# Expert rows of a two-block network: two gathers of 4 KB per row become one gather of 8 KB

## The chip, the core and the metric

The kernel runs on one core of a Trainium2 chip. The metric is the time of one execution on the device in microseconds; lower is better. Five engines run their own instruction streams and wait for each other by semaphores: TensorE (PE, matmuls), VectorE (DVE), ScalarE (ACT, activation functions), GpSimd (POOL, here only the issuer of gathers) and SyncE (SP, here only the issuer of plain transfers). Sixteen DMA engines move data between HBM and the on-chip buffers: `arena` (SBUF, 128 partitions) and `ps` (PSUM, the matmuls' accumulators).

## The reference

Two network blocks follow one another on 256 tokens of width 1024. The first has two layers; each mixes tokens (attention, a Fourier and a pooling branch, weighed by sigmoid gates) and then runs a layer of experts, in the first layer for 256 context tokens too. The second block has an attention and a recurrent mixer and one expert layer. Eight tiles of 128 tokens pass through an expert layer. For each token 128 of 16384 experts are chosen; an expert is a row of `peer_down` and a row of `peer_up`, 1024 numbers each:

```python
top_s, pos = lax.top_k(cand, PEER_TOPK)                   # 8 heads x 16 experts a token
eidx = jnp.take_along_axis(cidx, pos, axis=-1)
gate = jax.nn.softmax(top_s, axis=-1)
def one(args):
    hh, ee, gg = args
    a = jnp.einsum("tkd,td->tk", peer_down[ee], hh, preferred_element_type=jnp.float32)
    act = (gg * jax.nn.gelu(a)).astype(hh.dtype)
    return jnp.einsum("tk,tkd->td", act, peer_up[ee])
```

The gates of the mixer that the change also touches:

```python
g = jax.nn.sigmoid((zg + lp["b_gate"]).astype(jnp.float32)).astype(h.dtype)
g_a, g_b, g_c = jnp.split(g, N_BRANCH, axis=-1)
return (g_a * y_a + g_b * y_b + g_c * y_c) @ lp["w_out"], (k, v)
```

## The kernel before

The order of the work is written out by hand. The class `Walk` goes through the whole program; one subclass for each engine (`Vector`, `Tensor`, `Scalar`, `Pool`, `Sync`) goes the same way and issues its own instructions. `weave` lays two sequences into each other: the steps of a gather, and the units of other work (query projections, choice of experts for a later tile, the mixer of the next stage), about one unit (`RATE0` = 1.15) after each step. Since all engines walk the same interleaving, an instruction stands behind everything that its engine issues for earlier steps and units, and waits there for its own semaphores.

An expert layer is a **gather**. There are three: one of four tiles (two of the tokens, two of the context), and two of two tiles, 1024 rows in all. A **row** is one expert for each of the 128 tokens of a tile. Its down rows (128 x 4 KB) are fetched by one indirect DMA and its up rows by another. At step s:

- GpSimd (`Pool.gather`, DMAs recorded at L3075) fetches down row s into one of five buffers (`ND`), once VectorE is through with row s-5, then up row s-18 into one of five others (`NU`), once TensorE, and in odd tiles VectorE, are through with up row s-23 (`freed`).
- VectorE (`Vector.gather`, L906) waits for down row s and multiplies it by the tile's tokens, which lie in PSUM (`HP`), summing along the row: the **dot**, 128x1024 with an accumulator. After each 16 rows (`GK`) it multiplies 16 activated sums by the expert gates `GT`. In odd tiles it also does the **add** of row s-18 (`LAG`): the up row's second half times its weight, onto the sum `av` in PSUM, 128x512.
- ScalarE (`Scalar.gather`, L2462) takes gelu of 16 sums at a time, and for each row scales the identity by the row's weights into one of four 128x128 diagonals (`dg`).
- TensorE (`Tensor.gather`, L1701) multiplies the diagonal with the up row and accumulates into `ap` (first half), in even tiles into `av` too. Each such matmul leaves two records in the trace.
- At the end of a tile VectorE folds both sums, times a row of the modulation, into the tile (`fold`). In the last 18 steps of a gather no down rows are left, and up rows use all ten buffers.

The waits that tie these together, at L3052 and L3069:

```python
if s >= ND:
    self.wait_ge(S.down, c - ND + 1)
...
if i < 0:
    self.freed(max(0, u - NU + 1), total)
```

The gates of the mixer are ScalarE's sigmoids of matmul results, which VectorE multiplies with the branches.

## Time and profile before

| | |
|---|---|
| median of three runs | 4182.21 us (4175.77 to 4186.01) |
| span of the profiled execution | 4362.9 us |
| TensorE, VectorE, ScalarE, GpSimd busy in it | 77%, 59%, 19%, 47% |
| gathers: first indirect DMA of the first one | 446.77 us |
| queue q0 (GpSimd's transfers) | 1141.10 MB in 313344 packets |

The profiled execution is longer than the timed ones; its rows are read against its own span. The page gives each engine's busy time over the whole; the windows give the same for any stretch, with the granted clock of TensorE (1 is full speed) and what the DMA engines moved. The timeline shows single instructions with the idle time of their engine ahead of them and who ended it.

### The profile page before, as it was taken

How to read it: one execution, taken by the hardware profiler on the slowest of the kernel's cores; microseconds unless marked ns; L12 is line 12 of the kernel's file. 1: busy time of each engine (PE TensorE's matmuls, PEld its weight loads, DVE VectorE, ACT ScalarE, POOL GpSimd, SP SyncE). 2: the span in 40 equal slices, each digit the busy share in tenths (PEclk: the TensorE clock that was granted, in tenths of full speed). 3: DMA queues.
4: the chain of work that ended last, by engine and by line, in shares of the span. 5: the costliest groups of instructions: out<-in, count | busy, mean ns of one | idle time of the engine just before them, and what ended most of it. 6: DMA issues, size and time to landing. Idle time of an engine off the chain costs nothing.

```text
span 4362.9 us, 35889 instructions
## 1 busy us (share of the span) xinstructions
PE 3358.4 (77%) x11238; PEld 1715.0 (39%) x11238; DVE 2577.2 (59%) x5454; ACT 816.5 (19%) x1926; POOL 2040.9 (47%) x2148
## 2 busy tenths in 40 slices
PE   6889686888767787887687766766878887866766
PEld 2357442356434243551354422221366654422111
DVE  1412768566686846676357674666563347684776
ACT  1311111321211122121211111111231211111111
POOL 0210566655555666666116665566000005676665
PEclk9999899999979899996899988866988998999556
DMA  6663998999999999999849999999400039999999
GB/s 228 227 237 130 338 363 320 375 356 409 401 362 355 343 378 352 392 410 375 298 159 369 333 365 392 372 405 374 157 1 1 1 113 338 352 350 372 379 369 346
DMA packets 380787, 1330.31 MB, mean 305 GB/s; under 512 B 39500, under 2 KB 44876, under 8 KB 377016
## 3 DMA queue, kind: packets, MB, share of 16 engines
q0 software_dynamic: 313344, 1141.10, 69.3%
q1 hardware_dynamic: 61104, 164.18, 10.1%
q10 hardware_dynamic: 6152, 22.74, 1.4%
q8 instruction: 93, 1.52, 0.1%
q14 instruction: 94, 0.77, 0.1%
HBM read 1326.69 MB, written 1.17 MB: 304 GB/s over the span
## 4 chain that ended last, share of the span: by engine, by line
PE 15%; DVE 10%; DMA 9%; issue 7%; POOL 5%; another core or an unknown queue 3%; ACT 2%; ACTq 0%; DVEq 0%; POOLq 0%
PE ps L1701 15%; POOL arena L3075 5%; DMA arena<-in_peer_up,arena 5%; DVE arena L893 3%; DVE arena L906 3%; DMA arena<-in_peer_v,arena 2%; ACT arena L2462 1%; DMA arena<-in_ada_w 1%; DMA arena<-in_peer_u,arena 1%; DMA arena<-in_peer_down,arena 1%; PE ps L1707 1%; DVE arena L914 1%; DVE arena L1287 1%; DVE arena L1282 0%
## 5 line engine op out<-in xcount | busy, mean ns | idle before, releaser
L1701 PE MATMUL ps<-arena 128*128 128x512 f32 (+9 forms) x10500 | 3254.6, 490 | 873.9 <-ACT arena L2462 231.9
L1701 PEld LDWEIGHTS ps<-arena 128*128 128x128 f32 (+4 forms) x10500 | 1621.6, 196 | 2435.2 <-issue 1844.2
L906 DVE SCALAR_TENSOR_TENSOR arena<-arena,ps 128x1024 f32<-128x1024 f32 x1024 | 1240.6, 1217 | 542.1 <-DMA arena<-in_peer_down,arena 289.1
L3075 POOL DMA_INDIRECT arena<-in_peer_down,arena x768 | 747.1, 973 | 654.8 <-DVE arena L910 269.5
L3075 POOL DMA_INDIRECT arena<-in_peer_up,arena x768 | 736.5, 959 | 541.2 <-PE ps L1701 294.3
L2462 ACT ACTIVATE arena<-arena 128x128 f32<-128x128 f32 (+5 forms) x1242 | 444.4, 387 | 1890.8 <-PE ps L1701 636.3
L3075 POOL DMA_INDIRECT arena<-in_peer_u,arena x256 | 248.4, 970 | 647.9 <-DVE arena L910 543.6
L906 DVE SCALAR_TENSOR_TENSOR ps<-arena,ps 128x512 f32<-128x512 f32 x508 | 383.4, 755 | 143.0 <-DMA arena<-in_peer_up,arena 88.8
L2462 ACT ACTIVATE arena<-ps 128x512 f32<-128x512 f32 (+4 forms) x349 | 191.5, 549 | 1165.6 <-PE ps L1701 547.9
L3075 POOL DMA_INDIRECT arena<-in_peer_v,arena x256 | 242.4, 947 | 149.2 <-issue 59.9
L893 DVE TENSOR_TENSOR arena<-arena 128x512 f32<-128x512 f32 (+8 forms) x398 | 246.9, 620 | 72.1 <-ACT arena L2462 42.1
L893 DVE TENSOR_TENSOR arena<-ps,arena 128x512 f32<-128x512 f32 (+3 forms) x192 | 131.3, 684 | 254.8 <-PE ps L1701 220.8
L1707 PE MATMUL ps<-arena 128*128 128x128 f32 (+2 forms) x738 | 129.6, 314 | 124.5 <-DVE arena L893 68.5
L893 DVE TENSOR_TENSOR arena<-arena,ps 128x256 f32<-128x256 f32 (+1 forms) x134 | 73.0, 545 | 222.7 <-PE ps L1701 171.2
L1707 PEld LDWEIGHTS ps<-arena 128*128 128x128 f32 (+2 forms) x738 | 97.8, 157 | 205.8 <-issue 108.6
L2462 ACT ACTIVATE arena<-ps,arena 128x256 f32<-128x256 f32 (+2 forms) x140 | 71.2, 508 | 423.1 <-PE ps L1701 260.4
L910 DVE COPY arena<-ps 128x512 f32<-128x512 f32 (+5 forms) x69 | 39.6, 574 | 172.2 <-PE ps L1701 124.0
L2462 ACT ACT_TABLE_LOAD x81 | 103.9, 1283 | 56.1 <-DVE arena L893 29.8
L1277 DVE MAX8 arena<-ps 128x8 f32<-128x128 f32 x128 | 28.6, 288 | 137.9 <-PE ps L1701 98.7
L3021 POOL DMA_DIRECT2D arena<-in_w_mod x40 | 30.6, 765 | 132.0 <-PE ps L1701 69.6
L906 DVE DVE_READ_ACCUMULATOR arena<-arena,ps 128x1 f32 x1024 | 86.3, 84 | 0.0
L914 DVE TENSOR_REDUCE arena<-ps 128x1 f32<-128x512 f32 (+2 forms) x50 | 30.3, 607 | 81.9 <-PE ps L1701 69.4
(34 smaller groups left out, 565.1 us busy)
## 6 DMA issues: line engine op xcount, KB each, us to landing
arena<-in_w_mod POOLq DMA_DIRECT2D x40, 1024.0 KB, 6.6
arena<-in_gate_blocks SPq DMA_DIRECT2D x16, 2048.0 KB, 7.8
arena<-in_w_in SPq DMA_DIRECT2D x14, 2048.0 KB, 7.9
arena<-in_w_pq SPq DMA_DIRECT2D x13, 2048.0 KB, 16.0
arena<-in_ada_w POOLq DMA_DIRECT2D x24, 1024.0 KB, 8.3
arena<-in_w_out SPq DMA_DIRECT2D x8, 2048.0 KB, 8.0
arena<-in_gate_blocks SPq DMA_DIRECT2D x8, 1792.0 KB
arena<-mod_scratch ACTq DMA_DIRECT2D x26, 512.0 KB
```

The lines of the kernel that those rows point to most:

```text
L893: self.e.tensor_tensor(o, a, b, op).then_inc(*(inc or self.inc(self.S.vec)))
L906: self.e.scalar_tensor_tensor(o, a, s, b, op0, op1, accum_out=accum).then_inc(*(inc or self.inc(self.S.vec)))
L910: self.e.tensor_copy(o, a).then_inc(*(inc or self.inc(self.S.vec)))
L914: self.e.tensor_reduce(o, a, AX, op).then_inc(*(inc or self.inc(self.S.vec)))
L1277: e.max(v[j][:, 0:8], src[j]).then_inc(*self.inc(S.vec))
L1287: e.match_replace(tmp[j], v[j][:, 0:8], src[j], NEG).then_inc(*self.inc(S.vec))
L1701: return self.e.matmul(o, l, r, start=start, stop=stop)
L1707: ins = self.e.transpose(o, x, self.K.ident)
L2462: self.e.activation(o, i, f, bias=bias, scale=scale, accum_out=accum).then_inc(*(inc or self.inc(self.S.act)))
L3021: self.e.dma_start(K.sums[place].rearrange("p (k n) -> p k n", n=512), rows[:, 4 * half:4 * half + 4, :]).then_inc(S.sums_in[place], 16)
L3075: self.e.indirect_dma_start(out=o, out_offset=None, in_=table, in_offset=bass.IndirectOffsetOnAxis(ap=idx.bitcast(U32), axis=0)).then_inc( ...
```

## The change

The two tables are laid side by side, so that a row of the new table `peer_pairs` holds an expert's down row and up row, 8 KB; for the second block `peer_pairs_2`. One indirect DMA of 128 x 8 KB fetches both into one of six pair buffers (`NP`; 48 KB of a partition, where ten buffers of 4 KB were). A pair is free again when TensorE, and in odd tiles VectorE, are through with its up half. `LAG` falls from 18 to 1: matmul and add of row s-1 stand at step s. ScalarE therefore works row by row: gelu of 128x1, a copy scaled by the expert gate (VectorE's multiplication of 16 columns is gone; a new semaphore `gated` tells ScalarE that the gates are there), the diagonal. `LEAD` = 16 keeps the place where modulation rows are asked for. The fold writes into the row buffer and needs three instructions for four. The mixer's gates become 0.5 (1 + tanh(z/2)): ScalarE takes tanh with scale 0.5 and a halved bias, VectorE (1 + tanh) times the branch in one instruction of the same size, and the 0.5 goes into a later product. The arena is laid out anew and is 6 KB of a partition longer; GpSimd's descriptor scratch gives those up (2048 for 8192). Rates and units of the interleaving stay, apart from marks ("after") that follow the new lag. GpSimd has one gather DMA per row, 512, 256 and 256 in the three gathers, where it had twice as many; ScalarE has 99 table loads where it had 81.

```diff
-ND = NU = 5
-GK = 16
-LAG = GK + 2
+NP = 6
+LAG = 1
+LEAD = 16
...
-    def down_place(self, s):
-
-        x = self.base + LAG // 2 * self.gathers + s
-        return self.K.ds[x % ND], (self.S.down_in[x % ND], 16 * (x // ND + 1))
-
-    def up_place(self, u, total):
-
-        i = u - (total - LAG)
-        if i < 0 or i % 2 == 0:
-            x = self.base - LAG // 2 * self.gathers + (u if i < 0 else total - LAG + i // 2)
-            return self.K.us[x % NU], (self.S.up_in[x % NU], 16 * (x // NU + 1))
-        return self.down_place(total + i // 2)
+    def pair_place(self, s):
+
+        x = self.base + s
+        return self.K.pairs[x % NP], (self.S.pair_in[x % NP], 16 * (x // NP + 1))
...
-            yield ("after", 2 * NEXT + 6)
+            yield ("after", 2 * NEXT + LAG - 12)
...
+        self.ts(K.cols2[:, :, 0:24], K.cols2[:, :, 0:24], 0.5, None, M, None)
...
-                    self.tt(MX[:, j, :], gs[i], b.ap[:, 0:256], M, inc=self.drain(b))
+                    self.stt(MX[:, j, :], gs[i], 1.0, b.ap[:, 0:256], AD, M, inc=self.drain(b))
...
-                self.tt(ty, b.ap, g[:, 512 * c:512 * c + 512], M, inc=self.drain(b))
+                self.stt(ty, b.ap, 0.5, g[:, 512 * c:512 * c + 512], M, M, inc=self.drain(b))
...
-        self.tt(gt, gt, m["s8b"][:, hs].unsqueeze(2).to_broadcast([128, n, 16]), M)
+        self.tt(gt, gt, m["s8b"][:, hs].unsqueeze(2).to_broadcast([128, n, 16]), M, inc=self.inc(S.gated))
...
-                c = base + s
                 if k == 0:
                     self.wait_ge(*self.next(S.row_in_psum))
-                d, there = self.down_place(s)
+                pair, there = self.pair_place(s)
                 self.wait_ge(*there)
+                d = pair[:, 0:D]
                 self.stt(d, d, 1.0, K.HP, M, M, inc=self.inc(S.down), free=True, accum=K.AA[n % 2][:, k:k + 1])
-            if s >= GK + 1 and (s - 1) % GK == 0 and s - 1 <= total:
-                n_, g = divmod((s - 1) // GK - 1, NEXT // GK)
-                ks = slice(GK * g, GK * g + GK)
-                self.wait_ge(*self.next(S.activated))
-                w = K.AW[n_ % 2]
-                self.tt(w[:, ks], w[:, ks], K.GT[:, tiles[n_], ks], M, inc=self.inc(S.weighted), free=True)
-                self.weighted = self.own()
             u = s - LAG
             if u >= 0:
                 n, k = divmod(u, NEXT)
                 c = base + u
-                w = K.AW[n % 2][:, k:k + 1]
-                buf, there = self.up_place(u, total)
                 if n % 2:
-                    self.wait_ge(*there)
-                    if k % GK == 0:
-                        self.wait_ge(*self.weighted)
-                src = buf[:, 512:1024]
-                if n % 2 and self.halves(u):
-                    self.wait_ge(S.up_vector, self.halves(u))
-                if n % 2 == 0:
-                    pass
-                elif k == 0:
-                    self.wait_ge(S.tile_done, c // NEXT)
-                    self.ts(K.av, src, w, None, M, None, inc=self.inc(S.up_vector), free=True)
-                else:
-                    self.stt(K.av, src, w, K.av, M, AD, inc=self.inc(S.up_vector), free=True)
-                if k == NEXT - GK:
+                    src, w = self.pair_place(u)[0][:, D + 512:2 * D], K.AW[n % 2][:, k:k + 1]
+                    self.wait_ge(S.weighted, c + 1)
+                    if self.halves(u):
+                        self.wait_ge(S.up_vector, self.halves(u))
+                    if k == 0:
+                        self.wait_ge(S.tile_done, c // NEXT)
+                        self.ts(K.av, src, w, None, M, None, inc=self.inc(S.up_vector), free=True)
+                    else:
+                        self.stt(K.av, src, w, K.av, M, AD, inc=self.inc(S.up_vector), free=True)
+                if k == NEXT - LEAD:
                     gate = self.row()
                 if k == NEXT - 1:
                     self.fold(tiles[n], c, *gate)
         self.base += total
         self.shared += total // 2
-        self.gathers += 1
 
     def fold(self, t, c, n0, gr, g_in):
 
         K, S = self.K, self.S
         self.wait_ge(*g_in)
         self.wait_ge(S.up_tensor, c + 1)
-        self.tt(K.tpb, K.ap, gr[:, 0:512], M)
-        self.tt(self.X(t)[:, 0:512], self.X(t)[:, 0:512], K.tpb, AD)
-        self.tt(K.tpb, K.av, gr[:, 512:1024], M, inc=self.inc(S.sum_read))
-        self.tt(self.X(t)[:, 512:1024], self.X(t)[:, 512:1024], K.tpb, AD, inc=self.inc(S.tile_done))
+        self.tt(gr[:, 0:512], K.ap, gr[:, 0:512], M)
+        self.tt(gr[:, 512:1024], K.av, gr[:, 512:1024], M, inc=self.inc(S.sum_read))
+        self.tt(self.X(t), self.X(t), gr, AD, inc=self.inc(S.tile_done))
...
-                buf, there = self.up_place(u, total)
-                self.wait_ge(*there)
+                up = self.pair_place(u)[0][:, D:2 * D]
                 if k == 0 and c:
                     self.wait_ge(S.sum_read, c // NEXT)
-                ins = self.mm(K.ap, K.dg[c % 4], buf[:, 0:512], k == 0, k == NEXT - 1)
+                ins = self.mm(K.ap, K.dg[c % 4], up[:, 0:512], k == 0, k == NEXT - 1)
                 if n % 2 == 0:
-                    ins = self.mm(K.av, K.dg[c % 4], buf[:, 512:1024], k == 0, k == NEXT - 1)
+                    ins = self.mm(K.av, K.dg[c % 4], up[:, 512:1024], k == 0, k == NEXT - 1)
                 ins.then_inc(*self.inc(S.up_tensor))
...
-                self.act(g_, b.ap[:, 0:256], ACT.Sigmoid, bias=K.cols2[:, l, 8 * i + j:8 * i + j + 1], inc=self.drain(b))
+                self.act(g_, b.ap[:, 0:256], ACT.Tanh, scale=0.5, bias=K.cols2[:, l, 8 * i + j:8 * i + j + 1], inc=self.drain(b))
...
-            if s >= GK and s % GK == 0 and s <= total:
-                n_, g = divmod(s // GK - 1, NEXT // GK)
-                ks = slice(GK * g, GK * g + GK)
-                self.wait_ge(S.down, base + s)
-                self.act(K.AW[n_ % 2][:, ks], K.AA[n_ % 2][:, ks], gelu, inc=self.inc(S.activated))
-            if s < total and k == 0:
-                if base + s:
-                    self.wait_ge(S.down, base + s)
-                self.act(K.HP[:, 0:512], K.H2[:, tiles[n], 0:512], ACT.Copy)
-                self.act(K.HP[:, 512:1024], K.H2[:, tiles[n], 512:1024], ACT.Copy, inc=self.inc(S.row_in_psum))
-            u = s - LAG + 1
-            if 0 <= u < total:
-                n, k = divmod(u, NEXT)
-                c = base + u
-                if k % GK == 0:
-                    self.wait_ge(*self.next(S.weighted))
+            if s < total:
+                c = base + s
+                if k == 0:
+                    if c:
+                        self.wait_ge(S.down, c)
+                    self.act(K.HP[:, 0:512], K.H2[:, tiles[n], 0:512], ACT.Copy)
+                    self.act(K.HP[:, 512:1024], K.H2[:, tiles[n], 512:1024], ACT.Copy, inc=self.inc(S.row_in_psum))
+                if k in K.routed_at[tiles[n]]:
+                    self.wait_ge(*self.next(S.gated))
+                a, w = K.AA[n % 2][:, k:k + 1], K.AW[n % 2][:, k:k + 1]
+                self.wait_ge(S.down, c + 1)
+                self.act(a, a, gelu, inc=self.inc(S.activated), free=True)
+                self.act(w, a, ACT.Copy, scale=K.GT[:, tiles[n], k:k + 1], inc=self.inc(S.weighted))
                 if c >= 4:
                     self.wait_ge(S.up_tensor, c - 3)
-                self.act(K.dg[c % 4], K.ident, ACT.Copy, scale=K.AW[n % 2][:, k:k + 1], inc=self.inc(S.diagonal), free=True)
+                self.act(K.dg[c % 4], K.ident, ACT.Copy, scale=w, inc=self.inc(S.diagonal))
             u = s - LAG
-            if u >= 0 and u % NEXT == NEXT - GK:
+            if u >= 0 and u % NEXT == NEXT - LEAD:
...
-                c = base + s
-                if k in self.K.routed_at[tiles[n]]:
+                if k in K.routed_at[tiles[n]]:
                     self.wait_ge(*self.next(S.routed))
-                if s >= ND:
-                    self.wait_ge(S.down, c - ND + 1)
-                elif base:
-                    self.freed(0, total)
-                o, there = self.down_place(s)
-                self.fetch(o, down, K.EI[:, tiles[n], k:k + 1], there[0])
-            u = s - LAG
-            if u >= 0:
-                n, k = divmod(u, NEXT)
-                c = base + u
-                i = u - (total - LAG)
-                if i < 0:
-                    self.freed(max(0, u - NU + 1), total)
-                elif i >= ND + NU:
-                    self.freed(u - ND - NU + 1, total)
-                elif i % 2 == 0:
-                    self.freed(total - LAG + i // 2 - NU + 1, total)
-                else:
-                    self.wait_ge(S.down, base + total + i // 2 - ND + 1)
-                o, there = self.up_place(u, total)
-                self.fetch(o, up, K.EI[:, tiles[n], k:k + 1], there[0])
+                self.freed(max(0, s - NP + 1))
+                pair, there = self.pair_place(s)
+                self.fetch(pair, table, K.EI[:, tiles[n], k:k + 1], there[0])
         self.base += total
         self.shared += total // 2
-        self.gathers += 1
-
-    def freed(self, n, total):
+
+    def freed(self, n):
...
-    K.NB = NB = 53200
-    K.arena = arena = ctx.enter_context(nc.sbuf_tensor("arena", [128, NB + 2 * D], F32))
+    K.NB = NB = 52688
+    K.END = END = NB + 4 * D
+    K.arena = arena = ctx.enter_context(nc.sbuf_tensor("arena", [128, END], F32))
...
-    more = Mem(arena, (NB, NB + 2 * D))
-    K.ds, K.us = [gm(D) for _ in range(ND - 1)] + [more(D)], [gm(D) for _ in range(NU - 1)] + [more(D)]
+    tail = Mem(arena, (NB, END))
+    K.pairs = [gm(2 * D) for _ in range(4)] + [tail(2 * D) for _ in range(2)]
...
+    pair = lambda a, b: np.concatenate([np.asarray(inputs[k]).reshape(-1, D) for k in (a, b)], 1)
+    f["peer_pairs"], f["peer_pairs_2"] = pair("peer_down", "peer_up"), pair("peer_u_2", "peer_v_2")
...
-    nc = bacc.Bacc("TRN2", target_bir_lowering=False, num_devices=1, dynamic_dma_scratch_size=8192)
+    nc = bacc.Bacc("TRN2", target_bir_lowering=False, num_devices=1, dynamic_dma_scratch_size=2048)
...
```

What moved on ScalarE in the first gather, where the context attention is laid between the rows. The exps are `128x256`, `128x2x128` is a copy out of PSUM that belongs to them, a diagonal is `128x128`, the batch of 16 gelus `128x16`. Before:

```order
L2462 ACTIVATE arena<-ps 128x2x128
L2462 ACTIVATE arena<-ps,arena 128x256
L2462 ACTIVATE arena<-arena 128x128
L2462 ACTIVATE arena<-ps,arena 128x256
L2462 ACT_TABLE_LOAD
L2462 ACTIVATE arena<-arena 128x16
L2462 ACTIVATE arena<-arena 128x128 x2
```

After, where `128x1 x2` is the gelu and the weight of one row:

```order
L2438 ACTIVATE arena<-arena 128x128
L2438 ACT_TABLE_LOAD
L2438 ACTIVATE arena<-ps,arena 128x256
L2438 ACT_TABLE_LOAD
L2438 ACTIVATE arena<-arena 128x1 x2
```

The gelu stands between every two exps now, and each change of function has its table load.

What moved on VectorE at the end of the first gather. A dot is `arena<-arena,ps 128x1024`, an add `ps<-arena,ps 128x512`, the `TENSOR_TENSOR` rows behind them are the fold (the one of `128x16` is a batch's weights). Before:

```order
L906 SCALAR_TENSOR_TENSOR arena<-arena,ps 128x1024
L906 SCALAR_TENSOR_TENSOR ps<-arena,ps 128x512 x2
L893 TENSOR_TENSOR arena<-arena 128x16
L906 SCALAR_TENSOR_TENSOR ps<-arena,ps 128x512 x17
L893 TENSOR_TENSOR arena<-ps,arena 128x512
L893 TENSOR_TENSOR arena<-arena 128x512
```

After:

```order
L898 SCALAR_TENSOR_TENSOR ps<-arena,ps 128x512
L898 SCALAR_TENSOR_TENSOR arena<-arena,ps 128x1024
L898 SCALAR_TENSOR_TENSOR ps<-arena,ps 128x512 x2
L885 TENSOR_TENSOR arena<-ps,arena 128x512 x2
L885 TENSOR_TENSOR arena<-arena 128x1024
```

The adds that stood behind the last dot are two, where they were nineteen, and the fold follows at once.

## Rows read from the trace of the kernel before

**Rows 1.** Page, part 1: busy us (share of the span) x instructions.

```profile
PE 3358.4 (77%) x11238; PEld 1715.0 (39%) x11238; DVE 2577.2 (59%) x5454; ACT 816.5 (19%) x1926; POOL 2040.9 (47%) x2148
```

**Rows 2.** Windows, gather stages: us, busy us (x count) by engine, PEclk, DMA share, GB/s.

```profile
446.00:2070.00 1624.00, 1277.96 (x3730) 665.33 (x3730) 1094.45 (x2390) 321.77 (x809) 988.85 (x1024) 0.89 0.97 370
2268.00:3070.00 802.00, 573.49 (x1332) 234.30 (x1333) 517.97 (x1075) 124.04 (x314) 494.68 (x512) 0.81 0.97 370
3605.00:4363.00 758.00, 542.43 (x1216) 210.23 (x1216) 511.91 (x1058) 117.09 (x296) 490.77 (x512) 0.78 0.96 360
```

**Rows 3.** Windows, short stretches inside the gathers, same columns.

```profile
1000.00:1100.00 100.00, 87.41 (x320) 60.10 (x319) 67.95 (x115) 20.58 (x51) 60.03 (x64) 0.98 1.02 410
1400.00:1500.00 100.00, 73.05 (x164) 29.45 (x164) 86.78 (x284) 13.74 (x37) 65.73 (x67) 0.90 0.95 348
2915.00:2956.00 41.00, 30.01 (x33) 7.12 (x32) 31.80 (x50) 6.33 (x17) 27.83 (x31) 0.61 1.03 409
4100.00:4200.00 100.00, 70.84 (x72) 17.62 (x72) 70.72 (x110) 13.99 (x37) 66.23 (x71) 0.53 0.98 375
```

**Rows 4.** DMA queues at 1000:1100 us: packets, MB, share of 16 engines.

```profile
q0 software_dynamic: 8923, 32.50, 81.6%
q1 hardware_dynamic: 1472, 8.39, 20.5%
```

**Rows 5.** DMA queues at 1800:1900 us.

```profile
q1 hardware_dynamic: 609, 7.58, 18.2%
```

**Rows 6.** Timeline 4203 to 4206 us: start, us, instruction, [idle before <-releaser].

```profile
4203.23 1.22 DVE L906 SCALAR_TENSOR_TENSOR arena<-arena,ps 128x1024 f32<-128x1024 f32 x1 [1.45 <-issue]
4203.73 0.40 ACT L2462 ACTIVATE arena<-arena 128x128 f32<-128x128 f32 x1 [3.09 <-PE ps L1701]
4203.96 0.94 POOL L3075 DMA_INDIRECT arena<-in_peer_v,arena  x1 [0.98 <-PE ps L1701]
4204.37 0.08 DVE L906 DVE_READ_ACCUMULATOR arena<-arena,ps 128x1 f32 x1
4204.51 0.76 DVE L906 SCALAR_TENSOR_TENSOR ps<-arena,ps 128x512 f32<-128x512 f32 x1
...
4204.62 2.05 PE L1701 MATMUL ps<-arena 128*128 128x512 f32 x2 [1.44 <-ACT arena L2462]
...
4205.21 0.94 POOL L3075 DMA_INDIRECT arena<-in_peer_u,arena  x1 [0.30 <-issue]
```

**Rows 7.** Waits, GpSimd: us in total, times, longest us.

```profile
POOL arena L3075 <- PE ps L1701: 349.7, 230, 10.5
POOL arena L3075 <- DVE arena L906: 193.0, 178, 8.1
```

**Rows 8.** Timeline 446 to 452 us, start of the first gather.

```profile
446.77 1.03 POOL L3075 DMA_INDIRECT arena<-in_peer_down,arena  x1 [194.69 <-DVE arena L910]
...
451.30 1.22 DVE L906 SCALAR_TENSOR_TENSOR arena<-arena,ps 128x1024 f32<-128x1024 f32 x1 [1.22 <-DMA arena<-in_peer_down,arena]
```

**Rows 9.** Groups of ScalarE, shapes apart: busy us, mean ns, idle before.

```profile
L2462 ACT ACT_TABLE_LOAD x81 | 103.9, 1283 | 56.1 <-DVE arena L893 29.8 <-PE ps L1701 14.8 <-issue 3.6
L2462 ACT ACTIVATE arena<-ps,arena 128x256 f32<-128x256 f32 x88 | 41.8, 475 | 386.7 <-PE ps L1701 260.4 <-issue 65.0 <-remote 59.3
...
L2462 ACT ACTIVATE arena<-arena 128x1 f32<-128x1 f32 x68 | 13.8, 203 | 72.9 <-DVE arena L901 43.7 <-DVE arena L893 26.6 <-DMA arena<-in_cvec 0.8
...
L2462 ACT ACTIVATE ps<-arena 128x512 f32<-128x512 f32 x16 | 9.6, 602 | 0.5
...
L2462 ACT ACTIVATION_READ_ACCUMULATOR arena<-ps,arena 128x1 f32 x48 | 9.3, 193 | 0.0
```

**Rows 10.** Waits, VectorE, 446 to 2070 us.

```profile
DVE arena L906 <- DMA arena<-in_peer_down,arena: 147.1, 130, 6.5
...
DVE arena L1277 <- PE ps L1701: 38.2, 6, 9.5
```

**Rows 11.** Timeline 1030 to 1036 us, the gates' stretch.

```profile
1035.86 0.42 DVE L893 TENSOR_TENSOR arena<-arena,ps 128x256 f32<-128x256 f32 x1
```

59 lines of the change are left out of this document (26 added, 33 removed).

## The prediction

> **What bounds the kernel now.** I began with the busy line of the page: no engine is full over the span, TensorE with 77% leads [rows 1]. So the bound changes by stage. The windows by stage come next: three stages hold the 1024 gather rows (446 to 2070, 2268 to 3070, 3605 to 4363 us), 3184 us together, and in each the DMA engines are 96 to 97% busy while TensorE and VectorE are not [rows 2]. A busy share is not yet a rate, so short windows follow [rows 3]: the same full share carries 410 GB/s at 1000:1100 and 409 at 2915:2956, but 375 at 4100:4200 and 348 at 1400:1500, where VectorE is 87% busy with the expert choice. The reader is to see two kinds of rows: some at the DMA's best rate, and some where the buffers do not come back soon enough to hold it.
>
> One row is 1.0486 MB (128 x 8 KB), so at 409 GB/s it lasts 2.56 us. The bytes of the three stages are 1624 x 370 + 802 x 370 + 758 x 360 = 1170 MB; at 409 GB/s they would take 2860 us, so some 324 us of the 3184 lie above that floor.
>
> Everything is summed against the profiled execution of 4363 us. The median of the runs is 4182, 0.9586 of it; no row says where the 181 us lie, so I scale a change by 0.9586.
>
> **Part 1: 8 KB instead of twice 4 KB.** The bytes stay, so only what a packet costs beside its bytes can go. At 1000:1100 queue q0 (gather rows) took 81.6 us x 16 / 8923 = 146.3 ns per packet of 3642 B [rows 4]; at 1800:1900 queue q1 (weights, larger packets) took 18.2 x 16 / 609 = 478 ns per packet of 12,447 B [rows 5]. The line through both is 9.1 ns + 37.7 ns per 1000 B; q1 at 1000:1100 lies on it (223 ns for 5700 B; the line says 224). Two packets of 4096 B then take 327 ns and one of 8192 B takes 318: 2.8% less, 0.071 us per row, **-73 us** over 1024 rows. Bounds: 0, if the row still goes in two packets, and -73, since no row shows more.
>
> The Trainium skill (DMA: Bandwidth & Descriptors, section "Where 436 GB/s comes from") speaks against any gain: it gives about 358 GB/s as the core's share of HBM, and a limit on bytes does not move with packets. The trace disagrees: 409 to 410 GB/s from HBM [rows 3]. By that rule this term would be 0.
>
> **Part 2: one issue per row.** Before, each row costs GpSimd two indirect DMAs of 0.94 us, each followed by 0.30 us [rows 6]: 2.48 us, almost the 2.56 us of the transfer. After a stall it cannot catch up, and it stalls: 349.7 us in 230 waits for TensorE and 193.0 in 178 for VectorE [rows 7], always with the other stream queued behind the one that is stuck. After, an issue of the same kind takes 1.24 us per row. Twice the bytes per descriptor might make it longer; up to 2.5 us it would be hidden. What this returns is the part of the 324 us in which nothing else is late: the gather rows without other work, about 560 us (2900 to 3070, 3923 to 4013, 4050 to 4350), where 375 instead of 409 GB/s [rows 3] costs 8%: **-45 us**. The rows beside the expert choice are bounded by VectorE's own work and I give them nothing. Bounds: 0, and half of the 324, -162.
>
> **Part 3: six pairs, one row of lag.** A pair is held until the matmul of its row is done. First fetch at 446.77, first dot at 451.30: 4.5 us [rows 8]; the second half MB adds 1.28 us at 409 GB/s, so about 5.8 (an estimate). Then dot and its accumulator 1.31, gelu and weight 0.20 each [rows 9], diagonal 0.40, matmuls 2.05 at the low clock [rows 6], and 0.5 for hops: 10.5 us. Six buffers give 1.74 us per row, under 2.5, with 6 x 2.49 - 10.5 = 4.4 us to spare. Before, five down buffers had 5 x 2.56 - 5.8 = 7 us. So a pure row keeps the DMA's pace, and any hiccup beyond 4 us now idles the DMA where 6 to 7 were allowed. Price for pure rows: 0.
>
> **Part 4: the chain closes.** Before, gelu came once per 16 rows and ScalarE, TensorE and the addition worked 18 rows behind; VectorE could dot far ahead of the matmul. In the first gather it waits 147.1 us for the down rows and for TensorE only 6 times worth naming [rows 10]. After, the matmul of row s-1 needs dot s-1 through ScalarE, the other work's matmuls stand behind it in TensorE's order, their readers stand behind on ScalarE and VectorE, and the next dots behind those. As I read the order, this ring spans two rows. In the gates' stretch, 1000:1100, 32 rows in 100 us are 3.1 us per row; of 320 matmul records 64 belong to rows, so the others hold 87.4 x 256/320 = 70 us, 2.2 per row [rows 3]. The ring is dot 1.31 + ScalarE 0.80 + row's matmuls 1.05 + other matmuls 2.2 + VectorE's reader 0.42 [rows 11] + hops 0.5 = 6.3 us per two rows, 3.1 per row: exactly today's pace. In even tiles the row has four records, 0.9 us more, and 0.2 to 0.5 us per row are lost. I take **+20 us**; bounds 0 and +100.
>
> ScalarE itself gets three small instructions per row instead of one: 0.8 us of 2.5, hidden beside its 19% [rows 1]. Not hidden is the context attention: the order puts 16 exps between the rows' gelus, each now with a table load on either side. ScalarE's row there is 2 x 1.283 + 0.475 + 0.19 + 0.80 = 4.0 us against some 2.8: 16 x 1.2 = 19 us [rows 9]; with the ring through the scores' matmuls somewhat more. I take **+25 us**, bounds 0 and +50. In sum the program has 18 loads more (99 for 81), 23 us of ScalarE's time.
>
> First what the row shows: a load is 1283 ns [rows 9]. The Trainium skill (ScalarE: Activation LUTs, section "Table sets: the hidden batching unit") says to batch activations by table set, and names about 2.7 us for a switch; the trace has 1.28 for the load alone. The batches of 16 that are given up kept that rule. By 2.7 us the 32 loads of the attention would add some 45 us to my 25; the tanh gates keep it elsewhere.
>
> **Part 5: small things.** At a tile's end the two copies into PSUM (0.602 each [rows 9]) and the fold now follow the last dot at once instead of 18 rows apart: about 1 us on each of 8 tiles beyond the 4.4 us to spare. The three lead-outs lose their 17 rows of up fetches alone, but the bytes are the same. **+10 us**; bounds 0 and +25. Removed and on no path: 64 weight multiplications of 16 columns, four adds per fold to three. Gates by tanh: one VectorE form for another of the same size, 0.
>
> **Sum:** -73 - 45 + 20 + 25 + 10 = -63 us; 4363 - 63 = 4300; x 0.9586 = **4122 us**, 1.4% less.
>
> **Rivals.** (a) The rows go out no faster: an 8 KB row is moved as two 4 KB packets. For it: no packet of 8 KB on q0 is in the trace, only on q1. Then Part 1 is 0, and the sum +10 us, 4192: no change that can be told. The Trainium skill (DMA: Bandwidth & Descriptors, section "SWDGE vs HWDGE vs iDMA") states packets of at most 4096 B "preferably" on GpSimd's path; no row of before can show it.
>
> (b) **Slower**: the ring closes within one row. If the reader of TensorE's other work stands ahead of the next dot in the same step, the 6.3 us are paid per row, 3.2 more, in the gates' stretches (900 to 1150 and 1750 to 1990: 490 us, 158 rows). All of them would be +500; a quarter, as far as other units lie between and the 4.4 us of slack bridge it, is +125. Then -73 + 0 + 25 + 125 + 10 = +87, 4450 x 0.9586 = 4266. It decides from a fifth of those rows on (-73 - 45 + 35 + 100 is above zero). Against it: DMA share there is already full, and 3.1 us per row leave VectorE a third idle.
>
> (c) More is won: with GpSimd half idle and one stream, half of the 324 us comes back: -73 - 162 + 30 = -205, 4158 x 0.9586 = 3986. For it: VectorE waited for rows 130 times in the first gather alone [rows 10].
>
> **How the numbers follow.** Forecast 0.42 (own range 4080 to 4165), (a) 0.15, (b) 0.28, (c) 0.15. A measurement of this kernel can tell about 0.3%, 12.5 us. Faster: (c) and nearly all of the forecast, 0.55; same: most of (a), 0.15; slower: (b) and a rest of (a), 0.30. The range must reach both (b) and (c), 3985 to 4280.
>
> **What will show it.** q0's packets per MB halve if Part 1 holds, and the full windows read about 420 GB/s; GpSimd's busy time falls by a half, from 2041 to about 1080 us; windows of the last 300 us of gathers 2 and 3 go from 375 towards 410. ScalarE's loads read 99, and the stretch of the context attention is longer by some 25 us. Wrong would be: q0 still with packets of 4 KB; GpSimd's issue at 1.9 us; VectorE's dots waiting for TensorE in the gates' stretch, with the DMA share there under 0.9.

## The result, and the profile after

The changed kernel takes 4213.76 us (median of 4 runs) where the kernel before takes 4178.99: a ratio of 1.0082, 95% interval 1.0067 to 1.0098. It is **slower by 0.8%**, 35 us, and the interval excludes a ratio of 1, where 1.4% faster was forecast. The time lies inside the range of 3985 to 4280, but on the other side of no change.

The first part of the page of the changed kernel, and its largest DMA queue, beside [rows 1]:

```profile
PE 3334.9 (79%) x11238; PEld 1687.5 (40%) x11238; DVE 2541.6 (60%) x5383; ACT 1365.7 (32%) x3928; POOL 1050.5 (25%) x1124
...
q0 software_dynamic: 165888, 1141.03, 68.1%
```

GpSimd's busy time is halved and the packets of q0 fall from 313344 to 165888 with the same bytes, both as foretold. Yet the span of this execution, 4213.8 us, is *shorter* than the 4362.9 us of the trace that the prediction was read from. That alone says that the two traces can't be compared as they stand, so the kernel before was traced once more (first experiment below). That second trace has a span of 4177.6 us, what the timed runs take. From here on "before" is this second trace.

Windows, same columns as [rows 2]. The kernel before, second trace: rows 96 to 127 of the first gather (beside the context attention), the gates' stretch, and gather rows without other work:

```profile
714.00:812.00 98.00, 82.02 (x227) 38.89 (x227) 55.51 (x120) 34.43 (x91) 60.63 (x65) 0.87 0.92 346
965.00:1065.00 100.00, 87.30 (x326) 61.53 (x325) 68.21 (x116) 20.32 (x49) 60.60 (x65) 0.98 1.02 409
...
3985.00:4085.00 100.00, 72.21 (x78) 18.32 (x78) 76.66 (x121) 16.02 (x43) 72.50 (x78) 0.60 1.03 409
```

The changed kernel, the same three places:

```profile
738.00:864.00 126.00, 93.16 (x228) 41.71 (x229) 54.27 (x117) 85.84 (x179) 29.54 (x32) 0.86 0.76 281
1020.00:1120.00 100.00, 86.62 (x321) 59.23 (x320) 68.67 (x116) 33.32 (x108) 31.00 (x32) 1.00 1.01 418
...
4050.00:4150.00 100.00, 73.47 (x80) 17.84 (x80) 75.08 (x118) 35.42 (x118) 37.54 (x40) 0.62 1.01 420
```

Where the DMA sets the pace, the rate rises from 409 to 418 and 420 GB/s. The 32 rows beside the attention take 126 us instead of 98, and there the DMA's share falls from 0.92 to 0.76: it waits for buffers to come free. ScalarE is busy 86 us of these 126, where it was busy 34 of 98.

The first indirect DMA of each gather shows which stage lost (timeline; start, us, instruction, idle time of GpSimd before it). Before:

```profile
447.25 1.03 POOL L3075 DMA_INDIRECT arena<-in_peer_down,arena  x1 [194.99 <-DVE arena L910]
...
2186.81 0.99 POOL L3075 DMA_INDIRECT arena<-in_peer_down,arena  x1 [74.81 <-DVE arena L910]
...
3483.24 0.94 POOL L3075 DMA_INDIRECT arena<-in_peer_u,arena  x1 [545.66 <-DVE arena L910]
```

After:

```profile
448.74 1.03 POOL L3027 DMA_INDIRECT arena<-in_peer_pairs,arena  x1 [192.92 <-DVE arena L902]
...
2222.57 1.00 POOL L3027 DMA_INDIRECT arena<-in_peer_pairs,arena  x1 [74.77 <-DVE arena L902]
...
3518.33 0.94 POOL L3027 DMA_INDIRECT arena<-in_peer_pairs,arena  x1 [546.85 <-DVE arena L902]
```

From the first gather to the second: 1739.6 us before, 1773.8 after, +34. From the second to the third: 1296.4 and 1295.8. From the third to the end of the span: 694.4 and 695.5. The whole loss lies in the first gather, the one with the attention between its rows; in the other two the times hardly move, and e3 below shows that a gain and a loss cancel there.

How the loss comes about shows in 5 us of the changed kernel's timeline in that stretch (L1679 are TensorE's matmuls, L2438 is ScalarE, L898 the dot):

```profile
806.15 2.42 PE L1679 MATMUL ps<-arena 128*128 128x512 f32 x6 [2.37 <-ACT arena L2438]
806.17 1.28 ACT L2438 ACT_TABLE_LOAD   x1
...
807.47 0.47 ACT L2438 ACTIVATE arena<-ps,arena 128x256 f32<-128x256 f32 x1
...
807.84 0.19 ACT L2438 ACTIVATION_READ_ACCUMULATOR arena<-ps,arena 128x1 f32 x1
...
808.05 1.28 ACT L2438 ACT_TABLE_LOAD   x1
808.41 0.94 POOL L3027 DMA_INDIRECT arena<-in_peer_pairs,arena  x1 [3.64 <-PE ps L1679]
808.61 0.42 DVE L906 TENSOR_REDUCE arena<-ps 128x1 f32<-128x256 f32 x1 [3.23 <-PE ps L1679]
...
809.14 1.21 DVE L898 SCALAR_TENSOR_TENSOR arena<-arena,ps 128x1024 f32<-128x1024 f32 x1
809.35 2.07 ACT L2438 ACTIVATE arena<-arena 128x1 f32<-128x1 f32 x6
...
810.42 2.79 PE L1679 MATMUL ps<-arena 128*128 128x512 f32 x4 [1.85 <-ACT arena L2438]
```

TensorE's matmuls (a row's, and behind them the attention's scores) waited 2.37 us for ScalarE's diagonal. VectorE's maximum over the scores waited 3.23 us for TensorE. The next dot stands behind that maximum. ScalarE loads its table for the exp, loads it back for the gelu, and comes to the row only at 809.35; TensorE waits 1.85 us for it again. GpSimd waited 3.64 us for TensorE to give back a pair, so no fetch went out. No engine is full here; in these 5 us they wait for each other in a circle.

### The profile page after: what moved, and what is told of

It reads as the page before. It is cut to its first block, busy times and chain, and to the rows that moved or that the text cites. A ratio compares the mean times of both kernels' runs of the same rounds, so it can differ in the third digit from the quotient of the medians.

```text
span 4213.8 us, 36688 instructions
## 1 busy us (share of the span) xinstructions
PE 3334.9 (79%) x11238; PEld 1687.5 (40%) x11238; DVE 2541.6 (60%) x5383; ACT 1365.7 (32%) x3928; POOL 1050.5 (25%) x1124
## 3 DMA queue, kind: packets, MB, share of 16 engines
q0 software_dynamic: 165888, 1141.03, 68.1%
q1 hardware_dynamic: 61104, 164.18, 10.5%
## 4 chain that ended last, share of the span: by engine, by line
PE 19%; DMA 16%; DVE 11%; issue 3%; ACT 2%; ACTq 0%; POOL 0%; DVEq 0%; POOLq 0%
PE ps L1679 19%; DMA arena<-in_peer_pairs,arena 15%; DVE arena L885 4%; DVE arena L898 3%; ACT arena L2438 2%; DMA arena<-in_ada_w 1%; PE ps L1685 1%; DVE ps L898 1%; DVE arena L906 1%; DMA arena<-in_w_in 1%; DVE arena L1275 1%; DVE arena L1280 0%; DVE arena L1291 0%; DVE arena L1270 0%; DVE arena L1285 0%
## 5 line engine op out<-in xcount | busy, mean ns | idle before, releaser
L1679 PE MATMUL ps<-arena 128*128 128x512 f32 (+8 forms) x10500 | 3232.2, 488 | 756.0 <-ACT arena L2438 625.1
L1679 PEld LDWEIGHTS ps<-arena 128*128 128x128 f32 (+4 forms) x10500 | 1593.3, 194 | 2314.4 <-ACT arena L2438 1354.2
L898 DVE SCALAR_TENSOR_TENSOR arena<-arena,ps 128x1024 f32<-128x1024 f32 (+1 forms) x1096 | 1272.5, 1164 | 772.2 <-DMA arena<-in_peer_pairs,arena 630.2
L3027 POOL DMA_INDIRECT arena<-in_peer_pairs,arena x1024 | 983.7, 961 | 2826.7 <-PE ps L1679 1511.2
L2438 ACT ACTIVATE arena<-arena 128x1 f32<-128x1 f32 (+2 forms) x3226 | 969.0, 303 | 1656.2 <-DVE arena L898 1309.2
L2438 ACT ACTIVATE arena<-ps 128x512 f32<-128x512 f32 (+4 forms) x349 | 191.2, 548 | 870.9 <-PE ps L1679 609.1
L898 DVE SCALAR_TENSOR_TENSOR ps<-arena,ps 128x512 f32<-128x512 f32 x508 | 381.7, 751 | 73.1 <-ACT arena L2438 72.6
L885 DVE TENSOR_TENSOR arena<-arena 128x512 f32<-128x512 f32 (+8 forms) x326 | 234.5, 719 | 26.1 <-PE ps L1679 8.2
L2438 ACT ACTIVATE arena<-ps,arena 128x256 f32<-128x256 f32 (+2 forms) x140 | 71.1, 508 | 254.9 <-PE ps L1679 223.6
L885 DVE TENSOR_TENSOR arena<-arena,ps 128x512 f32<-128x512 f32 x62 | 42.6, 688 | 74.3 <-PE ps L1679 57.4
L898 DVE DVE_READ_ACCUMULATOR arena<-arena,ps 128x1 f32 x1024 | 84.3, 82 | 0.0
L906 DVE TENSOR_REDUCE arena<-arena 128x32 f32<-128x512 f32 (+7 forms) x64 | 54.6, 854 | 17.0 <-ACT arena L2438 15.1
L1291 DVE FIND_INDEX8 arena<-arena 128x8 uint32<-128x128 f32 (+1 forms) x192 | 59.9, 329 | 0.0
L1285 DVE MAX8 arena<-arena 128x8 f32<-128x128 f32 (+1 forms) x192 | 50.6, 325 | 0.0
## 6 DMA issues: line engine op xcount, KB each, us to landing
arena<-in_gate_blocks SPq DMA_DIRECT2D x16, 2048.0 KB, 10.5
```

The costliest lines, as they stand in the source:

```text
L885: self.e.tensor_tensor(o, a, b, op).then_inc(*(inc or self.inc(self.S.vec)))
L898: self.e.scalar_tensor_tensor(o, a, s, b, op0, op1, accum_out=accum).then_inc(*(inc or self.inc(self.S.vec)))
L906: self.e.tensor_reduce(o, a, AX, op).then_inc(*(inc or self.inc(self.S.vec)))
L1285: e.max(v[j][:, 8:16], tmp[j]).then_inc(*self.inc(S.vec))
L1291: e.max_index(ix[j][:, 8:16], v[j][:, 8:16], tmp[j]).then_inc(*(self.drain(b) if last else self.inc(S.vec)))
L1679: return self.e.matmul(o, l, r, start=start, stop=stop)
```

## The experiments

Medians of runs; each ratio is to the kernel before, timed on the same chip beside it.

| run | what is different | us | ratio (95%) |
|---|---|---|---|
| the change | | 4213.8 | 1.0082 (1.0067 to 1.0098) |
| e1 | no table loads between exps and gelus | 4184.0 | 1.0020 (1.0007 to 1.0033) |
| e2 | matmul and addition two rows behind | 4213.4 | 1.0090 (1.0073 to 1.0107) |
| e3 | two fetches of 4 KB rows | 4270.5 | 1.0233 (1.0216 to 1.0250) |
| e4 | five pairs | 4314.1 | 1.0309 (1.0277 to 1.0340) |
| e5 | diagonal written twice | 4269.8 | 1.0220 (1.0194 to 1.0246) |
| e6 | e1, and matmul independent of the dot | 4114.2 | 0.9848 (0.9832 to 0.9865) |
| e7 | gelu by tanh in 58 rows | 4235.9 | 1.0136 (1.0119 to 1.0153) |
| e8 | e6, pairs held a row longer | 4123.6 | 0.9878 (0.9862 to 0.9895) |
| e9 | before, gates by tanh | 4179.2 | 1.0001 (0.9991 to 1.0011) |
| e10 | matmul two behind, addition one | 4194.8 | 1.0041 (1.0027 to 1.0055) |
| e11 | e10 with a shorter chain | 4198.5 | 1.0049 (1.0032 to 1.0066) |
| e12 | e10 and e1 together | 4171.4 | 0.9985 (0.9973 to 0.9997) |
| e13 | e10 with exps two at a time | 4208.2 | 1.0066 (1.0049 to 1.0083) |

Where a run gains or loses shows by stage: us from the first indirect DMA of one gather to that of the next, and from the third to the end of the span, each in the run's own trace.

| run | first to second | second to third | third to the end |
|---|---|---|---|
| before, first trace | 1822.6 | 1336.1 | 757.4 |
| before, second trace | 1739.6 | 1296.4 | 694.4 |
| the change | 1773.8 | 1295.8 | 695.5 |
| e1 | 1751.5 | 1285.1 | 692.1 |
| e3 | 1797.1 | 1307.7 | 709.1 |
| e5 | 1806.0 | 1305.0 | 701.7 |
| e6 | 1706.8 | 1280.4 | 674.1 |
| e8 | 1715.5 | 1279.3 | 676.5 |
| e10 | 1757.8 | 1295.7 | 688.9 |

### The kernel before, traced again

> The kernel before, unchanged, for a second trace. Its profiled execution had a span of 4363 us where the timed runs take 4179. Theory A (that execution was held up, the gathers' pure rows at 375 GB/s were not typical): the new trace has about 4180 us, and windows of the last 300 us of the third gather read 405 to 410 GB/s, 2.56 us a row. Theory B (tracing always slows this kernel): about 4360 again, and 375 GB/s.

4179.45 us, span 4177.6, and 409 GB/s in the rows without other work (window 3985:4085 above) where the first trace showed 375 [rows 3]. Theory A holds. The 185 us by which the first trace was longer than this one lie in the three gathers, 83, 40 and 63 us of them (table above), and none ahead of the first. The rows from which a gain was counted are among them.

### e1: the table loads

```diff
-        table, gelu, gelu2 = A["peer_pairs"], ACT.Gelu_apprx_tanh, ACT.Gelu
+        table, gelu, gelu2 = A["peer_pairs"], ACT.Tanh, ACT.Tanh
```

> The changed kernel with tanh in the place of gelu in all three gathers (another function, so other numbers; the same instructions otherwise). Theory loads (the table loads between exps and gelus cost the time in the context attention): the table loads fall from 99 to about 65, rows 96 to 127 of the first gather fall from 4.0 to about 3.2 us each, and the whole gets 25 to 45 us shorter, 4170 to 4190. Theory ring (dot, ScalarE, matmul, other work, next dot in a circle): under 10 us shorter.

4184.0 us, 30 shorter than the change, as the theory of the loads had it; the loads fall to 38, further than expected, since others beside the expert choice go too. The window of rows 96 to 127:

```profile
737.00:841.00 104.00, 85.02 (x230) 39.24 (x231) 55.64 (x119) 50.21 (x151) 30.31 (x32) 0.92 0.85 335
```

104 us instead of 126: 22 of the 30 us come back here, beside the attention. The Trainium skill (ScalarE: Activation LUTs, section "Table sets: the hidden batching unit") asks for activations to be batched by set; the trace agrees, at 1.28 us per load, and the change gave that batching up.

### e2: everything a row later

```diff
-LAG = 1
+LAG = 2
```

> The changed kernel with the matmul and the addition two rows behind the dot instead of one. Theory ring: the circle now spans three rows, so stretches with other work speed up, 20 to 40 us shorter. Theory buffers (six pairs are too few, the DMA queues run dry): a pair is held a row longer, 2.5 us of the 4.4 us to spare are gone, 20 to 100 us longer.

4213.4 us, no difference: neither theory alone. The windows tell why. Rows 96 to 127 take 113 us instead of 126:

```profile
736.00:849.00 113.00, 83.06 (x231) 39.09 (x232) 54.65 (x117) 85.74 (x179) 29.46 (x32) 0.92 0.82 313
```

The circle is relieved here, and the same time is given back where the DMA sets the pace. Rows without other work:

```profile
4050.00:4150.00 100.00, 73.57 (x76) 18.10 (x76) 72.12 (x114) 34.07 (x114) 35.61 (x38) 0.58 1.00 401
```

401 GB/s, where the change has 420. In these odd tiles VectorE's addition now waits for a dot more before a pair is free; e10 puts only that addition back and has 418. Two effects of opposite sign had to be pulled apart (e8, e10).

### e3: 4 KB fetches in the changed kernel

```diff
...
-                self.fetch(pair, table, K.EI[:, tiles[n], k:k + 1], there[0])
+                self.fetch(pair[:, 0:D], table[0], K.EI[:, tiles[n], k:k + 1], there[0])
+                self.fetch(pair[:, D:2 * D], table[1], K.EI[:, tiles[n], k:k + 1], there[0])
...
```

> The changed kernel, but each row fetched by two DMAs of 4 KB packets from two tables into the two halves of the pair buffer; all else as in the changed kernel. If the 8 KB packets are worth 2.5% of the gathers' transfers and GpSimd's second issue hides, it is 50 to 75 us longer than the changed kernel (4265 to 4290), with 410 GB/s at best; if the packets give nothing, within 10 us of it.

4270.5 us, 57 more than the change. In rows without other work:

```profile
4100.00:4200.00 100.00, 77.60 (x78) 18.63 (x76) 73.61 (x117) 34.85 (x117) 72.64 (x78) 0.54 1.03 408
```

408 GB/s against 420. So the 8 KB rows with their single issue are worth 57 us, 23, 12 and 14 of them in the three stages of the table. Everything else in the change costs some 95 us over before.

### e4: five pairs

```diff
-NP = 6
+NP = 5
```

> The changed kernel with five pair buffers instead of six. The circle of one pair (fetch 5.8 us, dot 1.3, ScalarE 0.8, matmuls 2, hops 0.5 = 10.5 us) over five buffers is 2.1 us a row, still under the 2.50 of the transfer, with 2.0 us to spare instead of 4.5. Theory buffers: 40 to 120 us longer than the changed kernel, spread over all stretches with other work and the pure rows slower than 2.50 us. Theory ring (engines waiting for each other, whatever the buffers): under 20 us longer.

4314.1 us, 100 more than the change. Rows without other work:

```profile
4100.00:4200.00 100.00, 71.40 (x78) 17.53 (x78) 73.06 (x116) 34.57 (x116) 36.36 (x39) 0.62 1.00 407
```

Even these fall from 420 to 407 GB/s, 2.58 us a row. Five buffers in 2.58 us a row are a circle of 12.9 us per pair; my sum of unloaded parts gave 10.5. The trace tells which part is longer. From issue to the start of the dot it is 7.6 us on average in rows 900 to 999, where the sum had 5.8, and from the end of the dot to the next fetch into the pair 4.1, where it had 3.4. The row of the issues in that window, with the median from issue to landing as its last number:

```profile
arena<-in_peer_pairs,arena POOLq DMA_INDIRECT x39, 7.4
```

Six pairs then have about 6 x 2.50 - 12.9 = 2.1 us to spare, not 4.4. This is an estimate: the DMA's share is 1.00 in this window, so the 7.6 us can hold some waiting for the DMA itself. Buffers are scarce; whether they are what the changed kernel lacks, this run alone can't say, since a circle of engines that stalls also holds its buffers.

### e5: 0.4 us more in the chain

```diff
...
+                self.act(K.dg[c % 4], K.ident, ACT.Copy, scale=w)
                 self.act(K.dg[c % 4], K.ident, ACT.Copy, scale=w, inc=self.inc(S.diagonal))
```

> The changed kernel with each row's diagonal written twice by ScalarE, 0.4 us more between the dot and the matmul and nothing else. Theory ring: every row whose matmuls share TensorE with other work pays half of it or more, 20 to 60 us longer, pure rows unchanged at 2.50 us. Theory buffers: 0.4 of 4.4 us to spare, under 10 us longer.

4269.8 us, 56 more. The attention's rows, and rows without other work:

```profile
746.00:880.00 134.00, 91.14 (x229) 40.77 (x230) 54.74 (x118) 98.88 (x211) 29.90 (x32) 0.89 0.74 270
4100.00:4200.00 100.00, 73.50 (x81) 17.77 (x79) 75.10 (x121) 51.98 (x160) 36.71 (x40) 0.62 1.01 419
```

134 us instead of 126 in the first, 419 GB/s and 40 rows in 100 us, as in the change, in the second. The 0.4 us cost nothing where a row is alone; they cost where other work shares the engines, as the theory of the circle had it. But only 8 of the 56 us are in these 32 rows: by the table above the stages of the three gathers are 32, 9 and 6 us longer than in the change.

### e6 and e8: no circle, and pairs held without a circle

e6 has the edit of e1, writes the diagonal from a constant, one row ahead, and TensorE waits for the fetch instead of the diagonal's weight. The addition takes the constant too:

```diff
...
-                    src, w = self.pair_place(u)[0][:, D + 512:2 * D], K.AW[n % 2][:, k:k + 1]
-                    self.wait_ge(S.weighted, c + 1)
+                    src, w = self.pair_place(u)[0][:, D + 512:2 * D], 0.5
...
-                up = self.pair_place(u)[0][:, D:2 * D]
+                pair, there = self.pair_place(u)
+                self.wait_ge(*there)
+                up = pair[:, D:2 * D]
...
+                for d in ((0, 1) if s == 0 else (s + 1,)):
+                    if d < total:
+                        if base + d >= 4:
+                            self.wait_ge(S.up_tensor, base + d - 3)
+                        self.act(K.dg[(base + d) % 4], K.ident, ACT.Copy, scale=0.5, inc=self.inc(S.diagonal))
...
-                if c >= 4:
-                    self.wait_ge(S.up_tensor, c - 3)
-                self.act(K.dg[c % 4], K.ident, ACT.Copy, scale=w, inc=self.inc(S.diagonal))
...
+            self.wait_ge(self.S.down, self.base + n)
             self.wait_ge(self.S.up_tensor, self.base + n)
```

> The changed kernel with the dependence of the matmul and the addition on the dot taken out: diagonals and additions use the constant 0.5 in place of the weights (so the weights are left out of the result), the diagonal is written one row ahead, gelu is replaced by tanh as in the run before; gelu and weight are still worked out. A pair is given back when its dot, matmul and addition are done. Against the run with tanh alone (4184 us): theory ring: 40 to 65 us shorter, 4120 to 4145, the stretch of rows 96 to 143 under 2.8 us a row. Theory buffers: under 20 us shorter, since a pair is held only some 2 us less.

4114.2 us, 70 shorter than e1 and 64 shorter than before. Rows 96 to 127 are back at the pace of before:

```profile
732.00:831.00 99.00, 77.77 (x224) 36.68 (x224) 56.58 (x119) 47.40 (x151) 29.41 (x32) 0.91 0.85 336
```

But e1 has 104 us there already, so these rows hold only 5 of the 70. The rest shows by stage. The first indirect DMA of each gather in e1:

```profile
449.92 1.03 POOL L3027 DMA_INDIRECT arena<-in_peer_pairs,arena  x1 [193.62 <-DVE arena L902]
...
2201.47 1.00 POOL L3027 DMA_INDIRECT arena<-in_peer_pairs,arena  x1 [76.61 <-DVE arena L902]
...
3486.57 0.94 POOL L3027 DMA_INDIRECT arena<-in_peer_pairs,arena  x1 [543.72 <-DVE arena L902]
```

And in e6:

```profile
450.41 1.03 POOL L3031 DMA_INDIRECT arena<-in_peer_pairs,arena  x1 [195.38 <-DVE arena L902]
...
2157.25 1.00 POOL L3031 DMA_INDIRECT arena<-in_peer_pairs,arena  x1 [75.02 <-DVE arena L902]
...
3437.70 0.94 POOL L3031 DMA_INDIRECT arena<-in_peer_pairs,arena  x1 [541.60 <-DVE arena L902]
```

From the first to the second e6 is 45 us shorter than e1, from the second to the third 5, from the third to the end 18. So the dependence costs in gather rows beside all sorts of other work. An example are rows of the third tile beside the expert choice, 200 us from row 255 or so, first in e1 and then in e6:

```profile
1250.00:1450.00 200.00, 168.06 (x460) 81.66 (x460) 155.26 (x473) 65.28 (x222) 68.38 (x70) 0.97 0.98 394
...
1230.00:1430.00 200.00, 172.22 (x471) 84.16 (x472) 161.75 (x500) 60.06 (x225) 70.22 (x74) 0.98 1.01 409
```

e8 adds only that a pair waits for the next row's dot:

```diff
-            self.wait_ge(self.S.down, self.base + n)
+            self.wait_ge(self.S.down, self.base + n + (1 if n else 0))
```

> As the run without the chain (4114 us; constant 0.5 for the weights, tanh for gelu), but a pair is given back only when the dot of the following row is done too, about 2.5 us later, which is the time by which the chain holds it in the changed kernel. The engines still don't wait for each other. Theory buffers (holding the pairs is what costs): 40 to 70 us longer, near the 4184 of the run with tanh alone. Theory ring: under 20 us longer.

4123.6 us, 9 more. Rows 96 to 127:

```profile
732.00:830.00 98.00, 77.97 (x224) 36.70 (x224) 56.24 (x117) 47.36 (x150) 29.99 (x32) 0.91 0.89 349
```

Holding the pairs longer costs 9 us; the dependence of matmul on dot costs 70. But e8 doesn't hold them as long as e1 does. From the end of a dot to the next fetch into its pair it is 5.7 us on average in rows 144 to 383 of e1, 4.5 in e6 and 5.1 in e8; in rows 12 to 63 it is 5.4, 2.9 and 3.8. So e8 brings back between a third and somewhat over a half of the difference, and the holding could be put at 15 to 25 of the 70 us (an estimate that takes its cost as proportional). The larger part is then the engines waiting for each other; how the 70 us divide exactly is not shown. For the rows beside the attention e10 shows it better: pairs are held longer there than in the change, and the rows are faster.

### e7: gelu by tanh where the exps are

```diff
...
-                self.act(a, a, gelu, inc=self.inc(S.activated), free=True)
-                self.act(w, a, ACT.Copy, scale=K.GT[:, tiles[n], k:k + 1], inc=self.inc(S.weighted))
+                if base == 0 and 88 <= s < 146:
...
+                    self.act(cube, a, ACT.Square)
+                    self.act(line, a, ACT.Copy, scale=0.7978845608)
+                    self.act(cube, cube, ACT.Copy, scale=a)
+                    self.act(half, a, ACT.Copy, scale=K.GT[:, tiles[n], k:k + 1])
+                    self.act(cube, cube, ACT.Tanh, scale=0.0356774081, bias=line)
+                    self.act(half, half, ACT.Copy, scale=0.5, inc=self.inc(S.activated))
+                    self.act(w, cube, ACT.Identity, scale=half, bias=half, inc=self.inc(S.weighted))
...
```

> The changed kernel, but rows 88 to 145 of the first gather work out gelu by tanh, which shares the exps' table, in seven instructions of 128x1 instead of two; the same result. 32 table loads of 1.28 us go, 5 x 0.2 us per row come. Theory loads: rows 96 to 127 fall from 4.0 to about 3.4 us, 15 to 25 us shorter than the changed kernel, 4190 to 4200, still slower than before. If the ring's length in these rows is what counts rather than the loads: under 8 us.

4235.9 us: 22 longer, a miss. Its timeline of ScalarE in that stretch:

```profile
812.37 2.57 ACT L2438 ACTIVATE arena<-arena 128x1 f32<-128x1 f32 x8
```

Seven instructions of 128x1 and the diagonal of 0.40 are 2.57 us: 0.31 each where each waits for the one before, not 0.20. Seven make a chain of 2.2 us in all 58 rows, against two loads of 1.28 in the rows beside the 16 exps. The loads went (67 in the whole run, 99 in the change) and the chain grew, and the run is longer: the chain weighs more.

### e9: before, with the gates by tanh

```diff
...
-                self.act(g_, b.ap[:, 0:256], ACT.Sigmoid, bias=K.cols2[:, l, 8 * i + j:8 * i + j + 1], inc=self.drain(b))
+                self.act(g_, b.ap[:, 0:256], ACT.Tanh, scale=0.5, bias=K.cols2[:, l, 8 * i + j:8 * i + j + 1], inc=self.drain(b))
...
```

> The kernel before with the gates by tanh alone. 64 table loads instead of 81, in stretches that run at the DMA's rate: within 8 us of before.

4179.2 us, ratio 1.0001: no difference. In the kernel before, this part of the change is free and wins nothing by itself.

### e10 and e11: TensorE two rows behind

e10 lets only TensorE's matmul, and the fold, stand two rows behind; VectorE's addition keeps its place:

```diff
-LAG = 1
+LAG = 2
...
             u = s - LAG
             if u >= 0:
                 n, k = divmod(u, NEXT)
+                if k == NEXT - LEAD:
+                    gate = self.row()
+                if k == NEXT - 1:
+                    self.fold(tiles[n], base + u, *gate)
+            u = s - 1
+            if 0 <= u < total:
+                n, k = divmod(u, NEXT)
                 c = base + u
...
-                if k == NEXT - LEAD:
-                    gate = self.row()
-                if k == NEXT - 1:
-                    self.fold(tiles[n], c, *gate)
```

> The changed kernel with the matmul two rows behind the dot in TensorE's order (and the fold with it), the addition still one row behind. Where there is no other work TensorE starts at the same moment as before, so pairs are not held longer there; where there is, the circle spans three rows. Theory ring: 15 to 35 us shorter than the changed kernel, pure rows at 2.50 us. Theory buffers: within 10 us of it, since beside other work the pairs are held longer.

4194.8 us, 19 shorter than the change, as the theory of the circle had it. Rows 96 to 127 take 114 us, as in e2, and what e2 gave back elsewhere is kept:

```profile
735.00:849.00 114.00, 81.75 (x230) 38.62 (x231) 55.48 (x118) 85.58 (x179) 30.07 (x32) 0.92 0.82 316
...
4050.00:4150.00 100.00, 73.03 (x80) 17.54 (x80) 75.64 (x120) 35.49 (x119) 37.48 (x40) 0.64 1.01 418
```

In rows 96 to 127 a pair is fetched into again 7.9 us after the end of its dot, where it is 6.0 in the change: held longer, and still 12 us less for the 32 rows. So beside the attention it is not the holding that costs.

e11 shortens the chain on top:

```diff
...
+        self.act(K.dg[c % 4], K.ident, ACT.Copy, scale=K.GT[:, t, k:k + 1])
...
-                self.act(w, a, ACT.Copy, scale=K.GT[:, tiles[n], k:k + 1], inc=self.inc(S.weighted))
-                if c >= 4:
-                    self.wait_ge(S.up_tensor, c - 3)
-                self.act(K.dg[c % 4], K.ident, ACT.Copy, scale=w, inc=self.inc(S.diagonal))
+                self.act(K.dg[c % 4], K.dg[c % 4], ACT.Copy, scale=a, inc=self.inc(S.diagonal))
+                if n % 2:
+                    self.act(w, a, ACT.Copy, scale=K.GT[:, tiles[n], k:k + 1], inc=self.inc(S.weighted))
...
```

> As the run with the matmul two behind, and the chain from dot to matmul shortened by one instruction of ScalarE: the diagonal is scaled by the expert gate ahead of time (one more 128x128 copy per row, off the chain) and by the gelu in place; the product of gate and gelu is worked out in odd tiles only, for the addition. The chain is some 0.3 us shorter; from the run with the diagonal written twice (0.4 us more cost 56) it should be 20 to 45 us shorter than the run without it, if both directions weigh alike; if ScalarE's 0.4 us more per row bind in the attention's stretch, up to 10 us of that are lost.

4198.5 us, no shorter than e10 (the intervals overlap): a miss. What is off the chain still stands in ScalarE's order: the diagonal written ahead takes 0.4 us in front of the next row and waits there for TensorE three rows back. Which of the two eats the gain wasn't told apart.

### e12 and e13: is that all?

e12 is e10 with the edit of e1.

> The version with the matmul two rows behind (4195 us), with tanh in place of gelu (another function; no loads between exps and gelus). If loads and circle add up: 25 to 32 us shorter than it, 4163 to 4170, faster than before by 0.2 to 0.4%. If the longer lag already hides the loads: under 12 us shorter.

4171.4 us, 23 shorter than e10: most of the 30 us that the loads cost in e1 are still there with the longer lag. It is the only version with the circle closed that beats before, by 0.15%, and it computes another function.

e13 is e10 with two exps at a time:

```diff
...
-            if s < 16:
-                h, t = s // 2, s % 2
-                self.wait_ge(*self.next(S.row_max))
+            if s < 16 and s % 2 == 0:
+                first_held = held
+            if s < 16 and s % 2:
+                for x, b in ((s - 1, first_held), (s, held)):
+                    h, t = x // 2, x % 2
+                    self.wait_ge(*self.next(S.row_max))
...
```

> The version with the matmul two rows behind, with two exps of the attentions at a time, so that one pair of table loads serves both: 83 loads for 99, the same result. If loads count one by one, 16 x 1.28 = 20 us of ScalarE, and some 10 to 15 us of the whole, 4180 to 4185; if the exp that waits for its partner holds up the scores' banks, no shorter or longer.

4208.2 us, 13 longer than e10, although 16 loads are gone. Rows 96 to 127:

```profile
735.00:860.00 125.00, 90.15 (x232) 42.04 (x233) 63.69 (x122) 66.98 (x163) 31.15 (x32) 0.88 0.78 295
```

ScalarE has 19 us less to do in them (67 for 86) and they take 11 us more (125 for 114): as I read it, the circle pays for the wait of one exp for the other; no run tells this apart from the changed order as such. No version with the reference's result beat the kernel before.

## Why the prediction was wrong

**The base.** The first step that failed is Part 2, "-45", and under it one sentence: "no row says where the 181 us lie, so I scale a change by 0.9586". The term was the distance of 375 from 409 GB/s over 560 us of rows without other work. The second trace of before has 409 in such rows, so that distance was in one disturbed execution only and there was nothing to win in them. The first trace held a warning: at 2915:2956, in rows of the same kind, it reads 409 itself [rows 3]. Of the 324 us above the floor 185 were the disturbance, which takes more than half of what rival (c) counted on. What the single issue is worth beside other work is inside the 57 us of e3 and wasn't told apart.

**Part 1** was right. Forecast -73 us in the trace's terms, -70 scaled; measured -57 (e3 against the change), with the second issue's part in it. The queue in rows without other work, after, 4050:4150:

```profile
q0 software_dynamic: 5757, 41.93, 101.2%
```

101.2 us x 16 / 5757 = 281 ns per packet of 7283 B; the line through [rows 4, 5], 9.1 ns + 37.7 ns per 1000 B, says 284. The gain of 2.7% holds in rows which the DMA paces; that it is collected less beside the expert choice would explain 57 for 70, which isn't shown. Rival (a) falls: the packets did get larger. The Trainium skill (DMA: Bandwidth & Descriptors, section "SWDGE vs HWDGE vs iDMA") has packets of at most 4096 B "preferably"; this trace doesn't bear that out, since of the 5760 packets of that window only 639 are under 8 KB and the rate is 420 GB/s for 409.

**Part 3** was right for rows without other work: 40 rows in 100 us, 2.50 each, and 0.4 us more in the chain doesn't change it (e5). The reserve was sized wrong, 4.4 us for about 2, for the most part since a fetch among others takes 7.6 us and not 5.8 (e4).

**Part 4** holds the term that was mis-sized. The mechanism stood there, a circle over two rows through all engines. Its price was "+20 us; bounds 0 and +100"; e6 against e1 has 70, some of it by pairs held longer (e8). The loads were "+25 us; bounds 0 and +50"; e1 has 30. With Part 1 and Part 2 as measured and the other terms as forecast the sum is -57 + 0 + 20 + 25 + 10, about nothing; the 50 us by which the circle was priced too low are what makes the kernel slower. Measured, the sum is -57 + 0 + 70 + 30 = +43, against the +35 of the runs. It takes the effects as independent; the rest of -8, Part 5 among it, is little more than the 6 us by which the medians of before differ from one set of runs to another (4175.8 to 4181.7).

The place was wrong too, and not where the loss is easiest to see. Beside the attention the forecast was good: "longer by some 25 us", measured 28 (126 for 98), of which 22 go with the loads and 5 more with the dependence (e1, e6). With the loads kept, the longer lag of e10 brings 12 back, so part of their cost is paid through the circle. I worked the circle out for the gates' stretch, found it equal to the pace there, and the window of 1020:1120 bears that out (418 GB/s, 32 rows in 100 us). Of the rows beside the expert choice I wrote that they "are bounded by VectorE's own work and I give them nothing". There the circle costs: 394 GB/s in e1 and 409 in e6. By stage it is 45, 5 and 18 us in all, the attention's 5 and other rows among them. Two readings had made it look cheap. ScalarE's part was put at 0.80 us a row; two rows in the timeline above take 2.07, 1.03 each. And of VectorE's waits for TensorE before, the prediction names one line of [rows 10], 38.2 us in 6; the same view has more of them:

```profile
DVE arena L910 <- PE ps L1701: 25.6, 10, 6.6
...
DVE arena L893 <- PE ps L1701: 18.0, 9, 5.8
```

Which of the other work's instructions make the circle long in these rows stays open.

VectorE's waits, 446 to 2035 us after, beside [rows 10]:

```profile
DVE arena L898 <- DMA arena<-in_peer_pairs,arena: 279.0, 217, 6.4
DVE arena L902 <- PE ps L1679: 36.0, 16, 6.4
DVE arena L906 <- PE ps L1679: 33.4, 14, 5.0
```

The dots seem to wait for the DMA, 279 us. That is the name of the last link only. GpSimd's waits, whole span, beside [rows 7], give the link ahead of it:

```profile
POOL arena L3027 <- PE ps L1679: 1511.2, 740, 20.0
...
POOL arena L3027 <- DVE ps L898: 375.3, 198, 6.7
```

GpSimd waits for TensorE 740 times to give pairs back. Where the rate is full, as in 4050:4150 with 420 GB/s, that costs nothing; in 738:864, with 281, it does. The DMA's share alone doesn't tell the two apart: e2 and e4 have 401 and 407 GB/s at a share of 1.00.

**Rival (b)** had the right side and the wrong form: it put the loss into the gates' stretch, with the circle closed within one row, and 4266 us. In that stretch a row takes 3.1 us (32 in 100 us), and not the 6.3 of a circle within one row. That one row of lag more in TensorE's order brings the attention's rows from 126 us to 114 (e10) fits a circle over two rows, without counting its rows.

**Part 5** had no run of its own but for the gates, which are at 0 as forecast (e9). The new layout of the arena and GpSimd's smaller scratch had none either; they are in the rest of the sum.

## What to carry to other kernels

When the profiled execution is longer than the timed runs, find out where before counting a gain, or trace again: here the rows that the gain was read from were among the disturbed ones. A lag of many rows between engines is not idle slack; before it is cut, write down for each kind of neighbouring work the circle that the in-order engines then form, with the slowest reader in it, and compare it with the pace of that stretch. Instructions that leave a long chain one by one (a load, a copy) may not help when others come back in the order of the same engine (e7, e11).

## What the runs showed of the hardware

One execution of an unchanged program can run 4.4% longer than another (4362.9 and 4177.6 us of span), with the same instructions and 375 instead of 409 GB/s in gather rows. An indirect DMA of 128 x 8 KB takes GpSimd no longer than one of 128 x 4 KB: 0.961 us on average over 1024 after, 0.938 to 0.975 before. Instructions of 128x1 on ScalarE that wait for one another take 0.31 us each (e7), against a mean of 0.20 in [rows 9]. A DMA share of 1.00 or 1.01 went with 401 (e2), 407 (e4) and 420 GB/s (the change) in the same kind of rows, so the share doesn't show whether the rate is full.
